# A down block moved from behind two tiles to between two tiles, in the feed-forward of a two-layer streaming encoder

## The reference

```
def swiglu(x, w_gate, w_up, w_down):
    return (jax.nn.silu(x @ w_gate) * (x @ w_up)) @ w_down
...
    x = layer_norm(ALPHA * x + 0.5 * swiglu(x, lw['ffn1_gate'], lw['ffn1_up'], lw['ffn1_down']), g[0], b[0])
    mix, state = parallel_mixer(x, pos, a_past, rec[0], rec[1], rec[2], rec[3], rec[4], rec[5], lw)
    x = layer_norm(ALPHA * x + mix, g[1], b[1])
    x = layer_norm(ALPHA * x + cross_attention(x, mem_k, mem_v, lw['x_wq'], lw['x_wo']), g[2], b[2])
    x = layer_norm(ALPHA * x + 0.5 * swiglu(x, lw['ffn2_gate'], lw['ffn2_up'], lw['ffn2_down']), g[3], b[3])
```

## Time and profile before

| what | value |
|---|---|
| median of 3 runs | 2959.82 us (2950.83 to 2961.23) |
| profiled execution, its own time | 2964.56 us |
| its span, first to last instruction | 2962.7 us |
| TensorE busy | 2618.2 us, 88% of the span |
| VectorE, GpSimd, ScalarE busy | 1289.5, 1328.6, 602.6 us |

### The profile page before, as it was taken

The page is one execution under the profiler, slowest core; times in us unless marked ns, Lnnn a source line. Parts: engine busy times, 40 slices in busy tenths (PEclk is TensorE's granted clock), DMA queues, the critical chain, the costliest instruction groups (busy, mean ns, idle before and its releaser), DMA issues.

```text
span 2962.7 us, 47935 instructions
## 1 busy us (share of the span) xinstructions
PE 2618.2 (88%) x18582; PEld 2474.3 (84%) x18582; DVE 1289.5 (44%) x1698; ACT 602.6 (20%) x1165; POOL 1328.6 (45%) x816
## 2 busy tenths in 40 slices
PE   8999999898876699999999999998987866999996
PEld 8999999777665599999899999997776656999996
DVE  4332336635556632333433332366455366333234
ACT  1000015212314500000320000243023254000004
POOL 9555543312245455454475445343233344655531
PEclk9999999879987799999999999998999777999998
DMA  6322211102112122222132222111121121322210
GB/s 229 95 82 74 75 64 37 58 29 82 37 50 80 43 86 79 72 77 72 43 117 78 78 78 78 50 45 49 48 71 50 36 73 43 100 73 84 71 35 33
DMA packets 61006, 204.03 MB, mean 69 GB/s; under 512 B 6712, under 2 KB 13880, under 8 KB 60216
## 3 DMA queue, kind: packets, MB, share of 16 engines
q1 hardware_dynamic: 52192, 184.83, 19.6%
q10 hardware_dynamic: 8664, 17.17, 1.6%
HBM read 195.66 MB, written 7.88 MB: 69 GB/s over the span
## 4 chain that ended last, share of the span: by engine, by line
PE 76%; DVE 15%; issue 4%; ACT 3%; POOL 1%; DVEq 0%; ACTq 0%; DMA 0%; POOLq 0%
PE pairA L387 21%; PE pairB L387 17%; PE pairD L387 15%; PE pairD L396 10%; DVE h_lo L1514 3%; PE pairA L396 2%; PE pairB L396 2%; PE pairD L640 2%; PE pairD L642 1%; DVE scratch L1564 1%; DVE scratch L1510 1%; DVE y L1528 1%; ACT h_hi L1062 1%; DVE y L1553 1%; DVE pc L1946 1%
## 5 line engine op out<-in xcount | busy, mean ns | idle before, releaser
L2032 POOL TENSOR_SCALAR w<-w_raw 128x1024 fp32r<-128x1024 f32 x348 | 381.7, 1097 | 1265.5 <-issue 662.0
L2034 POOL TENSOR_TENSOR w<-w_raw,w 128x1024 fp32r<-128x1024 f32 x348 | 843.4, 2424 | 29.0
L387 PE MATMUL pairD<-h_hi,w 128*128 128x288 f32 x2688 | 509.3, 308 | 118.2 <-DVE y L1528 78.4
L387 PE MATMUL pairA<-x_hi,w 128*128 128x288 f32 x3136 | 564.0, 297 | 2.4 <-ACT pc L1152 2.4
L387 PEld LDWEIGHTS pairD<-h_hi,w 128*128 128x128 f32 x2688 | 421.0, 198 | 132.7 <-DVE y L1528 86.0
L387 PE MATMUL pairB<-x_hi,w 128*128 128x288 f32 x2752 | 494.6, 297 | 0.0
L387 PEld LDWEIGHTS pairA<-x_hi,w 128*128 128x128 f32 x3136 | 468.1, 189 | 4.5 <-ACT pc L1152 2.9
L387 PEld LDWEIGHTS pairB<-x_hi,w 128*128 128x128 f32 x2752 | 411.6, 189 | 0.9
L1510 DVE SCALAR_TENSOR_TENSOR scratch<-scratch,pairB 128x576 f32<-128x576 f32 x72 | 54.3, 755 | 743.1 <-PE pairB L387 743.1
L387 PE MATMUL pairA<-x_lo,w 128*128 128x288 f32 x1568 | 336.1, 296 | 0.0
L387 PE MATMUL pairD<-h_lo,w 128*128 128x288 f32 x1344 | 299.1, 305 | 0.0
(11 more groups left out here) (320 smaller groups left out, 3144.9 us busy)
## 6 DMA issues: line engine op xcount, KB each, us to landing
w_raw<-in_stream SPq DMA_DIRECT2D x348, 512.0 KB, 3.5
out_ak<-pa ACTq DMA_DIRECT2D x2, 1152.0 KB, 5.1
out_y<-y SPq DMA_DIRECT2D x2, 1152.0 KB, 4.9
mem_raw<-in_mem ACTq DMA_DIRECT2D x2, 1024.0 KB, 4.8
cst<-in_consts ACTq DMA_DIRECT2D x1, 1740.0 KB, 7.7
tb_dram<-in_rel ACTq DMA_DIRECT2D x2, 768.0 KB
y<-in_x ACTq DMA_DIRECT2D x2, 576.0 KB, 7.1
y<-in_x ACTq DMA_DIRECT2D x1, 1152.0 KB, 12.6
```

Source lines behind the costliest of these rows:

```text
L387: ins.append(mm(out[0:m, half, 0:n], wt, mv_[:, c:c + n], start=(start and i == 0), stop=(stop and i == 2)))
L2032: pool.tensor_scalar(hi, w_raw[:, j], 1.0, 0.0, ALU.mult, ALU.add).then_inc(unit_hi, 1)
L2034: pool.tensor_tensor(lo, w_raw[:, j], hi.bitcast(F32), ALU.subtract).then_inc(unit_split, 1)
```

## The change

TensorE's list: the first down block moves from ahead of tile 3 to between tiles 3 and 4, and in each half-round of the loop the down block moves from ahead of both tiles to between them. The weight stream is put in the same new order. Every down block still takes the same two tiles, from the same slots, and waits for the same count of finished products. The lists of VectorE, ScalarE, GpSimd and SyncE hold the same instructions in the same order as before.

```diff
--- before.py
+++ after.py
@@ -541,22 +541,24 @@
 
                 def ffn(fi, u0, x_stage, h0, before, j):
                     head(u0, x_stage, [(x, fi, f) for f in range(3) for x in "gu"], before)
-                    banks_read(D0, D1)
-                    down(u0 + 6, h0 + 5, ("d", fi))
                     banks_read(A, B)
                     uses[("ffn", fi, "A")], uses[("ffn", fi, "B")] = A.n, B.n
-                    for q in range(2):
-                        proj(u0 + 8 + 2 * q, A, ("g", fi, 3 + q))
-                        proj(u0 + 9 + 2 * q, B, ("u", fi, 3 + q))
+                    proj(u0 + 6, A, ("g", fi, 3))
+                    proj(u0 + 7, B, ("u", fi, 3))
+                    banks_read(D0, D1)
+                    down(u0 + 8, h0 + 5, ("d", fi))
+                    proj(u0 + 10, A, ("g", fi, 4))
+                    proj(u0 + 11, B, ("u", fi, 4))
                     a0, b0, d0, d1 = A.n, B.n, D0.n, D1.n
                     uses[("ffn", fi, "D0")], uses[("ffn", fi, "D1")] = d0, d1
                     with pe.Fori(0, BODIES) as i:
                         for m in range(2):
                             u = u0 + 12 + 6 * m
-                            down(u, h0 + 7 + 2 * m, None, 4 * i, 8 * i, (d0 + 4 * m, d1 + 4 * m), slot=2 - 2 * m)
-                            for q in range(2):
-                                proj(u + 2 + 2 * q, A, None, 12 * i, 4 * i, a0 + 2 * m + q)
-                                proj(u + 3 + 2 * q, B, None, 12 * i, 4 * i, b0 + 2 * m + q)
+                            proj(u, A, None, 12 * i, 4 * i, a0 + 2 * m)
+                            proj(u + 1, B, None, 12 * i, 4 * i, b0 + 2 * m)
+                            down(u + 2, h0 + 7 + 2 * m, None, 4 * i, 8 * i, (d0 + 4 * m, d1 + 4 * m), slot=2 - 2 * m)
+                            proj(u + 4, A, None, 12 * i, 4 * i, a0 + 2 * m + 1)
+                            proj(u + 5, B, None, 12 * i, 4 * i, b0 + 2 * m + 1)
                     for pair, k in ((A, 4), (B, 4), (D0, 8), (D1, 8)):
                         pair.n += k * BODIES
                     tail(u0 + FFN_UNITS - TAIL, fi, j, h0, ("ffn", fi))
@@ -2180,11 +2182,10 @@
                 cols(up, t * P)
 
         gate_up(0, 1, 2)
-        rows(down, 0)
-        gate_up(3, 4)
-        for m in range(1, 9):
+        for m in range(9):
+            gate_up(2 * m + 3)
             rows(down, m)
-            gate_up(2 * m + 3, 2 * m + 4)
+            gate_up(2 * m + 4)
         gate_up(FT - 1)
         rows(down, 9)
         rows(down, 10)
```

## The result

The changed kernel took 2878.12 us (median of 4, 2864.47 to 2884.32), the kernel before in the same comparison 2960.53. The ratio is 0.9691, with an interval of 0.9656 to 0.9726: 3.1% faster. The forecast was 2869, a ratio of 0.9693 to the median that it was made against. The profiled execution took 2884.32, 80.2 less than the one before.

A forecast was written before the change was run, and what follows sets the result against it. TensorE was taken to bound the kernel, pausing in its loops for VectorE's adds. 2964.56 - 93.9 (waits, slow restarts) + 3.2 (head's end) = 2873.9, less 4.7 to a median: 2869 us; range 2857 to 2893.

The forecast's parts named there:

- What bounds: In the four loops, TensorE's excess over its pace of 0.1333 us per matmul: 93.9 us to be had.
- The split of the 93.9: In the loops: 78.4 us of down blocks waiting for VectorE's adds, the other 15.5 mostly slow restarts behind 7 blocks.
- The new half-round: In the loop: adds meet nothing, own tiles cost no wait, first tile's product returns B with 4.7 us to spare.
- rival 1: In the loop, second up projections wait for B behind late adds; 64 us of the gain lost, 2933 us; chance 0.05.
- The head's end: Ahead of tile 3: a new wait of 0.6 us plus 0.2, four times, 3.2 us; upper bound 11.4.
- Weights: The reordered weight stream costs nothing: GpSimd needs 3.45 us per unit against 6.4 of TensorE, 54% busy.
- Rival 2: In feed-forwards without pauses the clock falls; gain gone at mean 0.94, 3075 us at 0.87; chance 0.03.
- Rival 3: Behind the feed-forwards, waits for weights or a transfer eat the gain; about 2960 us; chance 0.04.
- The median: Whole kernel: forecast median of 2869 us, 3.1% less than before; forecast case at 0.88.

The follow-up runs named there:

- head_only: Only the first down block of each feed-forward moved, loop as in the kernel before; ratio 1.0017 to the kernel before, median 2968.99 us.
- before_again: The kernel before the change, unchanged, profiled once more; one run, 2988.29 us.
- product_first: Changed kernel, but in VectorE's loop list the first tile's product stands ahead of the eight adds; ratio 0.9983 to the kernel before, 2956.11 us.
- late_7: Changed kernel plus two idle VectorE reductions (7.41 us) between the adds and the first tile's product; ratio 1.0071 to the kernel before, 2987.77 us.
- late_3: Changed kernel plus one idle VectorE reduction (3.75 us) between the adds and the first tile's product; one run, 2892.38 us.
- loop_only: Loop's down blocks moved as in the changed kernel, first down block as in the kernel before; ratio 0.9681 to the kernel before, 2866.99 us.

## Why the prediction was right

**What bounds: right.** 93.9 us were to be had in the loops by the pace of 0.1333 us per matmul; 95.2 came. The loops ran at 306.87 / 2304 = 0.1332.

**The split of the 93.9: right in kind.** The waiting of 78.4 recurred to the digit in head_only and before_again. The slow restarts did not: 7 blocks of 32 in the first profile, 12 in another of the same kernel, 13 in head_only, 4 in product_first, and 2 behind the 32 waits of late_7. The sum was made against the profile that had 7, so it fits that profile; another one of before would have given some 6 us more. The section of the Trainium skill that the prediction weighed ("TensorE: Matmul & The Clock Gate", psum-queue depth-cycling) is borne out in so far as the slow restarts came only behind pauses, and not as a rule for each pause.

**The new half-round: right.** The last add ended 0.8 us after its block, the product gave B back with 4.9 us to spare (4.7 forecast), the blocks' own tiles were never waited for. late_3 and late_7 show that this margin is real, and that rival 1 named the place that would decide; it only lacked a reason to come about.

**The head's end: right in kind, too small.** 3.2 us were forecast, 4.4 measured (after against loop_only): 0.87 of waiting and 0.24 of slow start (6.64 us for 48 matmuls instead of 6.40), four times. The missing quarter of a microsecond each is TensorE's own way back. The chain at the head's end shows it: VectorE is done at 53.72, TensorE goes on 0.32 us later.

```profile
49.97 3.21 PE pairB L396 x24
...
53.26 0.47 DVE scratch L1485
53.72 0.32 issue
54.04 6.64 PE pairA L387 x48
```

In rows 3 a pause ends within a few hundredths of a microsecond after the add. There the wait stands on the matmul itself; here it stands on a register instruction, with another wait between it and the first matmul (the rows of TensorE's order above). That this makes the difference was not tried by itself.

**Weights: right.** GpSimd was busy 165.4 of 306.9 us in a loop, 54%, and TensorE waited for it nowhere that it had not before.

**Rival 2, a clock that doesn't hold: didn't come.** It was 1.00 in all four loops without any pause. **Rival 3: didn't come either.** No wait behind the feed-forwards grew by more than 0.7 us. What grew in the first profile of after was the length of one stretch, at a lower granted clock (0.85, against 0.87 before); the third profile of the same kernel doesn't have it.

**The median.** 2869 forecast, 2878 measured. In the feed-forwards 90.0 us of the 90.7 came. It is luck that the two parts miss by nearly the same, 95.2 for 93.9 and 4.4 for 3.2. (The difference of these two is 90.8; the other 0.8 lies ahead of the fourth feed-forward's loop, where before ran a projection in 6.24 us instead of 6.40. Why it did is open.) The medians lie 82.4 apart. The 8 us between are less than the spread of the changed kernel's four runs (20 us, from 2864.47 at a mean granted clock of 0.942 to 2884.32 at 0.935); that they are the clock's course alone is not shown, since only one of the four was profiled.

## What to carry to other kernels

When an engine pauses in the middle of a block, look in the *other* engine's list at what stands ahead of the work that would release it: here TensorE waited for an add that stood behind a product the block didn't need. Either list can be mended, and the cheaper one may be the short one: three lines on VectorE did as much as moving 36 down blocks on TensorE. Wait for each buffer where it is used, not for all of them together, and measure the spare time of the new tightest place (4.9 us here), because it is what the next change will eat.

## What the runs showed of the hardware

- Pauses of 2.2 to 2.8 us were followed by a stretch at the lower clock only now and then: at 4 to 13 of the 32 blocks, and in late_7 at 2 of 32 up projections. The mean granted clock of the first 3 us was 0.50 to 0.76 behind these pauses and 1.00 behind the others. Such a restart cost 1.3 to 1.5 us, and four times (in head_only and before_again) 2.6 to 2.7. It doesn't look like plain chance which pauses it follows: the first pause of the second and of the fourth feed-forward, the two behind the long stretches at a low clock, had it in before, before_again, product_first and late_7, though not in head_only. What decides it stays open. The second feed-forward's first one in before_again and in late_7 (up projection, 8.14 us for 48):

```profile
1113.19 11.30 PE pairD L387 x72
```

```profile
1142.49 8.14 PE pairB L387 x48
```

- Outside the feed-forwards, where TensorE waits often, the same instructions take over 10 us more or less per layer from one execution to the next (layer 2: 638.2 to 650.1 for the three profiles of the changed kernel), with the granted clock at 0.87 to 0.85.
- The subtraction for a product's low part took 2.80 us beside GpSimd's subtraction and 0.76 where GpSimd happened to be idle. VectorE's and GpSimd's rows of late_3 show both cases, 124.62 and 133.21 on VectorE:

```profile
124.62 0.76 DVE L1516 TENSOR_TENSOR h_lo<-scratch,h_hi 128x576 fp32r<-128x576 f32 x1 [0.75 <-ACT h_hi L1064]
...
133.21 2.80 DVE L1516 TENSOR_TENSOR h_lo<-scratch,h_hi 128x576 fp32r<-128x576 f32 x1 [0.75 <-ACT h_hi L1064]
```

```profile
120.23 2.41 POOL L2038 TENSOR_TENSOR w<-w_raw,w 128x1024 fp32r<-128x1024 f32 x1
125.46 1.05 POOL L2036 TENSOR_SCALAR w<-w_raw 128x1024 fp32r<-128x1024 f32 x1 [2.83 <-PE pairB L387]
126.59 2.40 POOL L2038 TENSOR_TENSOR w<-w_raw,w 128x1024 fp32r<-128x1024 f32 x1
131.86 1.05 POOL L2036 TENSOR_SCALAR w<-w_raw 128x1024 fp32r<-128x1024 f32 x1 [2.87 <-PE pairA L387]
133.00 2.40 POOL L2038 TENSOR_TENSOR w<-w_raw,w 128x1024 fp32r<-128x1024 f32 x1
```

"SBUF — State Buffer" of the Trainium skill, section "Who interferes with whom", says that a VectorE instruction with two SBUF inputs contends with a GpSimd instruction that reads SBUF. These rows agree.

This bears on the pauses themselves. In before, the subtraction took 2.76 to 2.83 us ahead of all 32 pauses. GpSimd's rows beside rows 3 show why it met GpSimd there: TensorE releases both, and GpSimd's split of a unit begins at 133.38, 0.15 us after VectorE's product.

```profile
133.38 1.05 POOL L2032 TENSOR_SCALAR w<-w_raw 128x1024 fp32r<-128x1024 f32 x1 [2.87 <-PE pairD L387]
134.51 2.38 POOL L2034 TENSOR_TENSOR w<-w_raw,w 128x1024 fp32r<-128x1024 f32 x1
```

Without the 2.0 us that the subtraction takes longer here, a pause of 2.2 to 2.8 us would by estimate be one of 0.2 to 0.8 us. So another time for GpSimd's split is a third way to most of the gain; no run tried it.
